# Reordering the recurrence stage of a recurrent transformer block: input feed, early products, two half-array products

## The reference

```
xr, xw, xk, xv, xa, xg = h + (shift(h) - h) * mu[i]       # one mix of neighbouring tokens each
r, k, v = xr @ W_r, xk @ W_k, xv @ W_v                    # three 1024x1024 projections
w, a, g = decay, rate and gate, each from a small two-layer product
kk = normalised(k * k_k) per head;  k = k * (1 + (a - 1) * k_a)
S_t = S_{t-1} * w_t + (S_{t-1} @ -kk_t) (kk_t * a_t)^T + v_t k_t^T     # per head, 64x64 state
y_t = S_t @ r_t;  out = groupnorm(y) + (r * k * r_k).sum() * v, gated, projected
```

## Time and profile before

| | |
|---|---|
| median of 3 runs | 2600.11 us (2599.76 to 2603.5) |
| profiled run | 2599.76 us |
| its span | 2598.0 us |
| PE busy | 2506.1 us (96%) |
| DVE, ACT, POOL busy | 1190.2, 936.2, 1020.0 us |

### The profile page before, as it was taken

One profiled execution on the slowest core, in us unless ns is written; L12 is line 12 of the kernel. 1 busy time (PEld: TensorE's weight loads), 2 busy tenths in 40 slices (PEclk: granted clock), 3 DMA queues, 4 the chain that ended last, 5 costly groups with the idle time before them and its releaser, 6 DMA issues.

```text
span 2598.0 us, 32276 instructions
## 1 busy us (share of the span) xinstructions
PE 2506.1 (96%) x12188; PEld 1939.6 (75%) x12188; DVE 1190.2 (46%) x2017; ACT 936.2 (36%) x1580; POOL 1020.0 (39%) x618
## 2 busy tenths in 40 slices
PE   7999899999989999999999999999999899999997
PEld 5775478888845668886687788888767787888886
DVE  5113745213142675743724365164389533562462
ACT  3545643212245462223443323123333533322222
POOL 4331445444522232211562544345424443445344
PEclk9999799999989999988999999999999999999998
DMA  3222013333411110001332233332222221233231
GB/s 122 64 65 86 1 33 94 96 96 96 125 57 49 57 58 2 2 1 76 98 114 65 82 97 98 97 96 91 89 65 82 90 89 57 89 97 114 81 97 65
DMA packets 54416, 196.99 MB, mean 76 GB/s; under 512 B 6573, under 2 KB 6701, under 8 KB 53581
## 3 DMA queue, kind: packets, MB, share of 16 engines
q1 hardware_dynamic: 53312, 192.44, 23.7%
q10 hardware_dynamic: 974, 2.80, 0.3%
HBM read 193.12 MB, written 2.10 MB: 75 GB/s over the span
## 4 chain that ended last, share of the span: by engine, by line
PE 45%; DVE 6%; ACT 1%; issue 0%; POOLq 0%; POOL 0%; DVEq 0%; ACTq 0%
PE ps L387 11%; PE ps L389 11%; PE ps L388 11%; DVE ps L2850 4%; PE ps L375 3%; PE ps L376 3%; PE ps L377 3%; PE ps L2693 1%; PE ps L2716 1%; PE ps L2863 1%; DVE ps L3012 0%; PE ps L2461 0%; PE ps L2493 0%; PE ps L2703 0%; PE ps L2466 0%
## 5 line engine op out<-in xcount | busy, mean ns | idle before, releaser
L508 POOL TENSOR_TENSOR w_lo<-raw,w_hi 128x1024 fp32r<-128x1024 f32 x342 | 819.0, 2405 | 1003.3 <-ACT w_hi L481 1003.2
L387 PE MATMUL ps<-ahead_hi,w_hi 128*128 128x512 f32 x1216 | 481.8, 396 | 1.0 <-DVE ahead_lo L610 1.0
L389 PE MATMUL ps<-ahead_hi,w_lo 128*128 128x512 f32 x1216 | 474.0, 390 | 0.0
L388 PE MATMUL ps<-ahead_lo,w_hi 128*128 128x512 f32 x1216 | 473.8, 390 | 0.0
L481 ACT ACTIVATE w_hi<-raw 128x1024 fp32r<-128x1024 f32 x342 | 352.7, 1048 | 170.3 <-PE ps L377 91.1
L621 DVE TENSOR_TENSOR x_stream<-x_stream,ps 128x512 f32<-128x512 f32 x80 | 55.0, 688 | 467.3 <-PE ps L389 268.5
L387 PEld LDWEIGHTS ps<-ahead_hi,w_hi 128*128 128x128 f32 x1216 | 228.4, 188 | 52.4 <-issue 4.1
L388 PEld LDWEIGHTS ps<-ahead_lo,w_hi 128*128 128x128 f32 x1216 | 228.5, 188 | 50.8 <-issue 4.1
L389 PEld LDWEIGHTS ps<-ahead_hi,w_lo 128*128 128x128 f32 x1216 | 228.4, 188 | 47.5
L2984 ACT ACTIVATE ffn_s<-ps 128x512 f32<-128x512 f32 x44 | 26.4, 599 | 322.2 <-DVE ps L3012 322.2
L375 PE MATMUL ps<-ffn_a_hi,w_hi 128*128 128x512 f32 x352 | 137.6, 391 | 3.0 <-DVE ffn_a_lo L3017 2.9
(11 more groups left out here) (420 smaller groups left out, 4639.0 us busy)
## 6 DMA issues: line engine op xcount, KB each, us to landing
raw<-in_wall SPq DMA_DIRECT2D x346, 512.0 KB, 3.6
x_stream<-in_x SPq DMA_DIRECT2D x8, 256.0 KB, 7.5
cw<-in_cmp_w SPq DMA_DIRECT2D x1, 2048.0 KB, 8.1
out_y<-x_stream SPq DMA_DIRECT2D x8, 256.0 KB, 2.1
lora_a<-in_lora_a ACTq DMA_DIRECT2D x1, 1152.0 KB
dist<-in_consts SPq DMA_DIRECT2D x1, 1088.0 KB, 11.1
mem<-in_mem SPq DMA_DIRECT2D x1, 1024.0 KB, 6.4
gwb<-in_lora_b SPq DMA_DIRECT2D x1, 1024.0 KB
```

Source lines behind the costliest of these rows:

```text
L387: pe.matmul(out, hi, src.hi[:, t, 0:width], start=first, stop=False)
L388: pe.matmul(out, hi, src.lo[:, t, 0:width], start=False, stop=False)
L389: return pe.matmul(out, lo, src.hi[:, t, 0:width], start=False, stop=last)
L508: e.tensor_tensor(self.w.lo[:, s, :], self.raw[:, s, :], as_float(self.w.hi[:, s, :]), ALU.subtract).then_inc(lo_r.sem, 1)
```

## The change

Five edits, all in the order of work:

1. The feeds issue `base(m + n)` right after `rounded(m)`, from m = 0, and not one step later (and `mix` after `rest` in the same way).
2. In the queries stage `heads_sum(7)` and `cumulate(0)` move from the end of tile 0 to its middle, `cumulate(1)` from the middle of tile 1 to the end of tile 0, and the last bonus but one to the end of tile 7, where `early_products(0)` was.
3. In the values stage `spread(7)` and the last bonus come in tile 0, and the early products at the ends of tiles 0 to 4 in groups (0), (1, 2), (3, 4), (5, 6), (7). Odd pairs use PSUM banks 6 and 7, even ones 4 and 5, so that a product waits for the gather before last. The bonus rows are copied out in tile 0.
4. `t32` is issued ahead of `l32`, and the waits on ACT are adapted.
5. `g_tensor` and `seed_y` go through `range(8)`: four matmuls of one half, then four of the other.

The diff:

```diff
--- before.py
+++ after.py
@@ -1645,22 +1645,20 @@
         if 0 <= t - KD + 1 + feed.n < feed.n:
             feed.base(act, t - KD + 1 + feed.n)
         if t == KD - 1:
-            feed.rounded(act, 0)
-            for m in range(1, KD - 1):
+            for m in range(KD - 1):
                 feed.rounded(act, m)
-                if m - 1 + feed.n < KD:
-                    feed.base(act, m - 1 + feed.n)
+                if m + feed.n < KD:
+                    feed.base(act, m + feed.n)
 
     def next_vector(self, v, feed, t):
 
         if 0 <= t - KD + 1 + feed.n < feed.n:
             feed.mix(v, t - KD + 1 + feed.n)
         if t == KD - 1:
-            feed.rest(v, 0)
-            for m in range(1, KD):
+            for m in range(KD):
                 feed.rest(v, m)
-                if m - 1 + feed.n < KD:
-                    feed.mix(v, m - 1 + feed.n)
+                if m + feed.n < KD:
+                    feed.mix(v, m + feed.n)
 
     def heads_sum(self, pe, m):
         c = HEAD_TILES * 2 - 2 - 2 * m
@@ -1735,10 +1733,13 @@
                             stop=(p == KD - 1)), "bonus_sums")
 
     def queries_middle(self, pe, t):
-        if t == 1:
-            self.cumulate(pe, 1)
         if t:
             self.spread_tensor(pe, t - 1)
+            return
+        self.heads_sum(pe, KD - 1)
+        self.wait(pe, "rates", KD)
+        self.wait(pe, "decays", KD)
+        self.cumulate(pe, 0)
 
     def cumulate(self, pe, p):
         k = self.k
@@ -1750,16 +1751,9 @@
         self.done(mm, "cumulated")
 
     def queries_tensor(self, pe, t):
-        if t == 0:
-            self.heads_sum(pe, KD - 1)
-            self.wait(pe, "rates", KD)
-            self.wait(pe, "decays", KD)
-            self.cumulate(pe, 0)
-        elif t + 1 < KD:
+        if t + 1 < KD:
             self.cumulate(pe, t + 1)
-        if t == KD - 1:
-            self.early_products(pe, 0)
-        elif t:
+        if t:
             self.bonus_tensor(pe, t - 1)
 
     def grow(self, act, p):
@@ -1835,40 +1829,43 @@
         done(v.tensor_tensor(cut(B_), cut(B_), Em[:, :, 1:P + 1], ALU.mult), "vec")
 
     def values_middle(self, pe, t):
-        if t == 1:
+        if t == 0:
             self.spread_tensor(pe, KD - 1)
-        for p in ((), (2,), (), (5,), (7,), (), (), ())[t]:
-            self.early_products(pe, p)
 
     def values_vector(self, v, i, j):
         if i == 0 and j == 0:
             self.scaled_vectors(v, KD - 1)
 
     def values_tensor(self, pe, t):
-        if t < 2:
-            self.bonus_tensor(pe, KD - 2 + t)
-        if t == 2:
+        if t == 0:
+            self.bonus_tensor(pe, KD - 1)
             self.wait(pe, "vec", 4 * KD - 3)
-        for p in ((1,), (3,), (4,), (6,), (), (), (), ())[t]:
+        for p in ((0,), (1, 2), (3, 4), (5, 6), (7,), (), (), ())[t]:
             self.early_products(pe, p)
+
+    def early_bank(self, p):
+        return 6 if p % 2 else 4
 
     def early_products(self, pe, p):
 
         k, wait = self.k, self.wait
         if p == 0:
             wait(pe, "grown", 2 * KD)
+        elif p == 1:
+            wait(pe, "key_normed", KD)
+            wait(pe, "bonus_kept", 1)
         else:
-            wait(pe, "gathered", 4 * p)
+            wait(pe, "gathered", 4 * (p - 1))
         wait(pe, "vec", 4 * p + 4)
         for q in self.ORDER:
             i, o = q % NB, self.half(q // NB)
-            mm = pe.matmul(k.ps[:, 4 + q // NB, self.chunk(i)], self.rate[o, p, self.chunk(i)],
+            mm = pe.matmul(k.ps[:, self.early_bank(p) + q // NB, self.chunk(i)], self.rate[o, p, self.chunk(i)],
                            self.RA[o, 1, p, self.chunk(i)], start=True, stop=True)
         self.done(mm, "early_products")
 
     def gather(self, act, p):
 
-        k = self.k
+        k, bank = self.k, self.early_bank(p)
         blocks = self.q0 if p < 4 else self.q3
         at = slice(8 * (p % 4), 8 * (p % 4) + 8)
         self.wait(act, "early_products", p + 1)
@@ -1878,7 +1875,7 @@
         for g in range(4):
             s = slice(32 * g, 32 * g + 32)
             self.done(act.activation(blocks[s, :, at].rearrange("p t u -> p u t"),
-                                     k.ps[s, 4:6, :].rearrange("p b (u t) -> p (b u) t", u=4)[:, :, s], ACT.Copy),
+                                     k.ps[s, bank:bank + 2, :].rearrange("p b (u t) -> p (b u) t", u=4)[:, :, s], ACT.Copy),
                       "gathered")
 
     def values_scalar(self, act, i, j):
@@ -1887,14 +1884,12 @@
         if t == 0:
             fed = self.feed_v.handed
             act.wait_ge(fed.sem, fed(KD))
-        for p in ((0,), (2,), (), (5,), (7,), (), (), ())[t]:
-            self.gather(act, p)
         act.wait_ge(self.v_used.sem, self.v_used(t + 1))
         act.activation(self.vv[:, t, :], k.ps[:, j, :], ACT.Copy).then_inc(self.v_free.sem, 1)
-        for p in ((1,), (3,), (4,), (6,), (), (), (), ())[t]:
-            if p == 4:
-                wait(act, "bonus_sums", KD)
-                done(act.activation(self.bonus[0:2 * KD, :], k.ps[0:2 * KD, 7, :], ACT.Copy), "bonus_kept")
+        if t == 0:
+            wait(act, "bonus_sums", KD)
+            done(act.activation(self.bonus[0:2 * KD, :], k.ps[0:2 * KD, 7, :], ACT.Copy), "bonus_kept")
+        for p in ((0,), (1, 2), (3, 4), (5, 6), (7,), (), (), ())[t]:
             self.gather(act, p)
 
 
@@ -1955,7 +1950,6 @@
         k, wait, done = self.k, self.wait, self.done
         if p == 0:
             wait(pe, "gathered", 4 * KD)
-            wait(pe, "bonus_kept", 1)
             pe.wait_ge(self.v_free.sem, self.v_free(KD + RING))
         else:
             wait(pe, "bonus_out", p)
@@ -2053,13 +2047,13 @@
         wait(pe, "u32_taken", 2 * p + 2)
         wait(pe, "masked", 16 * p + 16)
         for q in range(8):
+            mm = pe.matmul(k.ps[:, 3 + q // 4, (q % 4) * P:(q % 4 + 1) * P], self.U[:, q, :], self.Tt[:, q, :],
+                           start=True, stop=True)
+        done(mm, "t32")
+        for q in range(8):
             mm = pe.matmul(k.ps[0:64, 7, 64 * q:64 * q + 64], self.Tt[0:64, q, 0:64], self.U[0:64, q, 0:64], start=True,
                            stop=True)
         done(mm, "l32")
-        for q in range(8):
-            mm = pe.matmul(k.ps[:, 3 + q // 4, (q % 4) * P:(q % 4 + 1) * P], self.U[:, q, :], self.Tt[:, q, :],
-                           start=True, stop=True)
-        done(mm, "t32")
 
     def u64_tensor(self, pe, p):
         k, wait, done = self.k, self.wait, self.done
@@ -2082,7 +2076,7 @@
     def g_tensor(self, pe, p):
         k, wait, done = self.k, self.wait, self.done
         wait(pe, "t64_taken", p + 1)
-        for q in self.ORDER:
+        for q in range(8):
             i, o = q % NB, self.half(q // NB)
             mm = pe.matmul(k.ps[o, 7, self.chunk(i)], self.AT[:, i, o], self.Tt[:, q, :], start=True, stop=True)
         done(mm, "g_sums")
@@ -2195,7 +2189,7 @@
         wait(act, "u32", p + 1)
         wait(act, "zeroed", 4)
         if p:
-            wait(act, "t32", p)
+            wait(act, "l32", p)
         sums = k.ps[:, 6, :].rearrange("p (u t) -> p u t", u=8)
         for r, c in ((32, 0), (96, 32)):
             done(act.activation(self.U[r:r + 32, :, 2 * c:2 * c + 32], sums[r:r + 32, :, c:c + 32], ACT.Copy), "u32_taken")
@@ -2213,7 +2207,6 @@
         wait(act, "placed", 8 * p + 8)
         done(act.activation(self.Tb[32:64, :, 0:32], k.ps[32:64, 7, :].rearrange("p (u t) -> p u t", u=8)[:, :, 0:32],
                             ACT.Copy), "l32_taken")
-        wait(act, "t32", p + 1)
         for r in (0, 64):
             done(act.activation(self.Tt[r:r + 32, :, r + 32:r + 64].rearrange("p (b u) t -> p b u t", b=2),
                                 k.ps[r:r + 32, 3:5, :].rearrange("p b (u t) -> p b u t", u=4)[:, :, :, r + 32:r + 64],
```

## The result

The changed kernel takes **2636.1 us** (median of 4 runs, 2634.33 to 2641.42) against 2600.06 before: a ratio of 1.0139, 95% interval 1.0126 to 1.0151. It is 36 us slower; 25.5 were forecast, and the time lies 0.1 us above the stated range.

A forecast was written before the change was run, and what follows sets the result against it. PE bounds the pair loop, the ACT and DVE round the queries, the solve u32. 15.0 + 0.5 + 7.8 + 2.5 = 25.8 on 2599.76, stated as 2625.5 us; own range 2620 to 2631, 8 in 10: 2613 to 2636.

The forecast's parts named there:

- Feed: Queries' feed: bases become a chain of 2.19 us a step, moving the second exponential and the stage's end +2.9 us.
- Start of values: Ahead of values tile 0: PE pauses 9.0 us for DVE's t, with the bonus now standing before the tile.
- Solve and u32: Late fourth gather delays the solve's end and u32 by +15.0 us, to 1014.5; PE waits some 4 us.
- Edit 5: Pair loop, g and seed_y: each group takes 1.58 us instead of 1.09, +7.8 us over eight pairs.
- Edit 4: Pair loop, t32 ahead of l32: u64's wait for ACT's copy is bare only in the first pair, +0.5 us.
- The clock: Half clock after new pauses: +2.5 us ahead of values tile 0, nothing ahead of u32; bounds 0 and 8.
- (c): Rival: both new pauses cost more clock, with later slow stretches in the pair loop too; 2631 to 2636 us, chance 0.11.
- theory T: Follow-ups' theory, pair loop: long PE runs on small products without a full-array one lower the clock; e7 expected 3 to 10 us gained.

The follow-up runs named there:

- e1: Kernel before with only g_tensor and seed_y going through range(8), four matmuls of one half, then four of the other: 2603.29 us, ratio 1.0029.
- e16: Kernel before with kv and the bonus product exchanged in the pair loop, plus the halves in a row in g and seed_y: 2594.68 us, ratio 0.9978.
- e2: Kernel before with only t32 issued ahead of l32: 2607.16 us, ratio 1.0044.
- e5: Changed kernel with l32 ahead of t32 again: 2627.4 us, ratio 1.0102 to the kernel before.
- e3: Kernel before with only the feed change, each base issued directly behind its rounding: 2608.1 us, ratio 1.0035.
- e4: Kernel before with only the queries and values reorderings (earlier sums and cumulates, bonus ahead of values tile 0, grouped early products): 2616.27 us, ratio 1.0074.
- e6: Changed kernel with the halves alternating again in g and seed_y: 2629.41 us, ratio 1.0112 to the kernel before.
- e11: Changed kernel with the feed's bases issued one step behind again: 2631.3 us, ratio 1.0134 to the kernel before.
- e12: Changed kernel with the bonus products of tiles 6 and 7 behind values tiles 0 and 1 again: 2635.84 us, ratio 1.0151 to the kernel before.
- e13: Kernel before with t32 ahead of l32 and the halves in a row, queries and values as before: 2611.5 us, ratio 1.0045.
- e9: Kernel before with l32 put between the first four and last four products of t32: +2.8 us by the medians, ratio 1.0025.
- e10: Kernel before with seed_kv and the bonus product exchanged in the pair loop, first pair unchanged: 2588.04 us, ratio 0.9963.
- e14: Changed kernel with seed_kv and the bonus product exchanged in pairs 1 to 7: 2616.58 us, ratio 1.0062 to the kernel before.
- e17: Kernel before with kv and the bonus product exchanged in the pair loop, plus t32 ahead of l32: 2594.2 us, ratio 0.9978.
- e15: Kernel before with kv and the bonus product exchanged in the pair loop and in the first pair too: 2587.35 us, ratio 0.9948.
- e7: Kernel before with seed_kv moved from behind t64 to between u64 and the bonus product: 2621.45 us, ratio 1.0085.
- e8: Kernel before with t32 ahead of l32 and seed_kv moved between u64 and the bonus product: 2620 us, ratio 1.0067.

## Why the prediction was wrong

- **Feed**: right. 2.19 us a step forecast, 2.20 measured; +2.9 at the second exponential forecast, +3.0 measured.
- **Start of values**: right. Pause of 9 us with DVE's t as releaser, 9.03 measured; bonus at 945.0 (942.1 + 2.9) forecast, 945.1 measured. Half clock behind it, 2.5 us lost forecast, 2.3 measured (4.6 us of work at 0.50).
- **Solve and u32**: right. 17.5 us with the clock forecast, 17.0 measured. PE waited for it 2.4 us and not 4. The solve itself took 35.3 us for 36.1, 0.8 less where 0.9 was estimated; whether POOL's work beside it is the reason no run shows.
- **Edit 5**: right in kind and size. 7.8 forecast, 0.97 to 0.98 a pair measured in clean pairs (e1, e16), which is 7.8 for eight.
- **Edit 4**: the step that failed. "I cost it at nothing; for p = 0 nothing does: **+0.5**". As a wait that is right: 0.47 us at u64 in the first pair, none in the others (e2). But the edit cost 7.7 us by the medians alone (e2) and 8.7 in the changed kernel (e5), through the clock, which I did not look at there.
- **The clock**: "**+2.5** for the first and nothing for the second". The first was right. The second was not: PE now waits 1.6 us for DVE's mask at 1011.7 and 2.4 ahead of u32, the clock falls between the two (1013.7), and half clock in the first period grew from 10.2 to 18.6 us, that is some 4 us of time. It is there without edit 4 too (e5: 33.7). For the rest of the pair loop the sum has no clock term at all.
- **The miss in figures**: the pair loop's 17.6 us are 7.8 of products, 0.5 of the wait and 9.3 of clock (half of 52.7 less 34.1). The sum had the first two. Together with the 1.9 behind the loop this gives the whole: 17.0 + 17.6 + 1.9 = 36.5, against 36.0 between the medians and 25.5 forecast. That these two agree within 0.5 is partly luck, since executions of either kernel differ by more.
- **Rivals**: (c) named this outcome ("later stretches of the pair loop too", 2631 to 2636), with new pauses as the mechanism. For the first period that fits, though no run isolates it. For the steady loop it doesn't: e2 has none of these pauses, and its clock falls in every period.

The rows to see it stood in the trace: before, one period was 25.5 us at 1.00 and the next 27.0 at 0.94, with the same products. It can be read as a loop on the edge, in which a change of order moves the clock and not only the products. I bounded the clock at 8 us and spent none of it on the loop.

What is shown, with one profile for each version. Of the seven periods these ran below full clock: with l32 ahead of t32, four before and in e1, e3, e5, and five in e4; with t32 ahead, all in e2, e6, e11, e12 and the changed kernel, and six in e13; with l32 in the middle, six in e9. With the exchange of kv and the bonus product it is the first alone in e10, e14, e16 and e17, with and without edits 4 and 5, and none in e15. Edit 4's cost in time is clear of the noise (e2, e5), and so is the gain by the exchange (e10, e14). The falls behind the first pair begin 10 to 12 us behind the pair's u32 in before, e2 and the changed kernel, that is around the bonus product and t64.

What stays open is the condition itself. An unbroken row of small products (theory T) explains e2, but not e9's profile nor e13's third period. The exchange moves two products at once, so no run tells whether kv between u64 and t64 or the bonus product behind t64 does it. e3 and e4, which leave the pairs' order alone, had long stretches in the loop as well, as before has: so a part of the clock's cost depends on when the loop starts or on chance, which no run here separates.

## What to carry to other kernels

Read the granted clock of a tight loop period by period before pricing a change in it: if equal periods differ, a change of the order of PE's products can cost more than their durations say (here 8 us against 0.5). Try to put a full-array product between small ones, and keep every copy that PE waits for covered by some product. The first without the second was dear here (e7, 21 us slower); both together gained 11 us (e10). Two matmuls on different halves of the array should be issued in turn.

## What the runs showed of the hardware that was not expected

- A wait of 0.68 us of PE, behind products that use a quarter of the array, was followed by 10 us at half clock and the period was 5.5 us longer than without it (e7: 30.8 for 25.3 in e10). In e8 the same wait was so followed in four pairs of six.
- The clock fell from full to half while PE was busy without a pause for 5.84 us (e2).
- Sixteen records of two halves in a row take 1.58 us, between 1.09 in turn and 2.05 for the whole array (e16; the other two in the earlier trace rows). The second half's first record starts ahead of the first half's last three.
